# A hybrid decoder layer on one core: a third PSUM bank in the expert stage, rounded slot weights, later LayerNorm rows, and TensorE waits for its own last matmul

## The chip, the cores and the metric

The kernel runs on one core of one Trainium2 chip (trn2). The metric is the device time of one execution in microseconds; before the change it is the median of three timed runs. One more execution was recorded by the hardware profiler; its times are read below.

## The reference, cut to what matters

One decoder layer on 256 tokens of 2048 channels, all in float32:

```python
u = x @ w_in                      # conformer GLU | q k v | short conv | 3 gates
a   = silu(LN(conv31(a_val * sigmoid(a_gate))))
att = dilated window attention over 3 patterns, merged by softmax denominators
c   = cb * conv3(cc * ch)
merged = sum_n sigmoid(g_n) * (branch_n @ w_branch[n])
x = LN(alpha * x + merged @ w_out)
# MoE: 64 SwiGLU experts of width 256, sigmoid scores, 4 of 8 groups, top 8, one shared expert
x = LN(alpha * x + moe(x))
```

## The kernel before, in words

All engines run their own instruction streams; semaphores set the order, which is written out by hand. `x_hi`/`x_lo`, `h_hi`/`h_lo`, `y_hi`/`y_lo` and `w_hi`/`w_lo` are a float32 value rounded to float32r and the rest that the rounding leaves; products of such pairs stand for a float32 product.

**The mixer** (to about 1200 us). SP loads weights in 2 MiB pieces into two buffers `raw` (L491), ScalarE rounds them (L640), VectorE subtracts for the rest (L921), and TensorE multiplies. The work is 200 *units* in eleven segments (`qk0`, `v0`, `aval`, `agate`, `qk1`, `v1`, `cc`, `ch`, `cb`, `gb`, `out`). A unit is 16 pairs of one 512-column and one 256-column matmul (L1494 and L1495, or L1485 and L1487, L1468 and L1469). Its last matmul increments `s_mm`; before a unit TensorE waits for the split (`s_lo`) and a free PSUM bank (`s_ev`). `multiply` holds this; the first iteration of each segment is written out, the others run in a hardware loop. Matmul instructions are queued, so TensorE normally runs from one unit into the next. Attention and two channel sums of the conformer branch are placed between units of `aval`, `cc`, `ch` and `cb`.

At the segment `out`, POOL waits for `s_mm` at `BASE_OUT`, loads x into `acc` (L597), waits until `merged` is split (`s_mlo` 4), and then issues the broadcasts of the LayerNorm's gain and bias rows (L599, L600), the router bias, and two small tables. VectorE needs the rows in `normalize`.

**The experts** (from about 1261 us). Pairs of experts (p), two pairs to a *quad* (q), 16 quads, and at the end a *job* (one more pair for experts that have over 64 tokens; more jobs only where needed). Each pair has six weight units of 2 MiB in a ring of six buffers: four gate and up units (`gate_up`, L1711), two down units (`down`, L1744). SP issues a load (L521) when TensorE has finished the unit that held the slot. Per quad TensorE does, in this order:

1. gate and up of the first pair into `ps_proj[0]`;
2. combine of the quad before (`combine`, L1762): its rows, rounded and rest, spread to the tokens by a 0/1 matrix, in two halves of four chunks of four matmuls; VectorE adds each chunk to `acc` (L1286);
3. between the halves the transposes of the hidden rows (`turn_hidden`, L1721), after them those of the selection (`turn_select`, L1726);
4. down of the first pair into `ps_s`;
5. gate and up of the second pair into `ps_proj[1]`;
6. gather of the next quad's tokens (`gather_part`, L1664) in two halves of four chunks of eight matmuls, each copied out by ScalarE (L794), with `turn_hidden` between them;
7. the slot weights (`slot_weights`, L1673): selection transposed times the four routing weights, in float32, copied out by VectorE (L1261);
8. down of the second pair.

PSUM has `ps_proj` (2 banks), `ps_s` (4 banks) and `ps_t` (2 banks, `swing[0]` and `swing[1]`). Everything of steps 2, 3, 6 and 7 goes through the two banks of `ps_t`, so each takes its turn after the others' readers (`s_acc`, `s_xt`, `s_ht`, `s_spreadt`).

Of the kernel before, what the change touches and what calls it, by code (L numbers as in the profile page):

```python
# [5 lines left out]
P = 128  # L6
# [45 lines left out]
def build(nc, x, w_in, conv_a_w, conv_a_b, ln_a_g, ln_a_b, conv_c_w, w_branch, w_out, ln1_g, ln1_b,  # L52
# [29 lines left out]
    with ctx:  # L82
# [95 lines left out]
        quad_w = at("quad_w", [P, TT, 4], F32, 197.25)  # L178
        slot_w = at("slot_w", [P, 2], F32, 197.28125)
# [32 lines left out]
        def gather_swing(t):  # L212


            return t % 2 if t < 4 else (t + 1) % 2
# [331 lines left out]
        def _(pool):  # L547
# [50 lines left out]
            pool.wait_ge(s_mlo, 4)  # L598
            pool.dma_start(ln_g[:, :], ln1_g.to_broadcast([P, D])).then_inc(s_lnp, 16)  # L599
# [17 lines left out]
        def _(act):  # L617
# [172 lines left out]
            def take_gathered(q, first):  # L790

                for t in range(first, first + 4):
                    act.wait_ge(s_gathered, 8 * q + t + 1)
                    nc.scalar.activation(xt[:, 2 * t:2 * t + 2, :].rearrange("p a c -> p (a c)"), swing[gather_swing(t)],  # L794
                                         ACT.Copy).then_inc(s_xt, 1)
# [14 lines left out]
            def take_spread(n):  # L810

                act.wait_ge(s_spread, n + 1)
                nc.scalar.activation(spread_t[:, :, :], swing[1].rearrange("p (k c) -> p k c", k=2),
# [12 lines left out]
            take_gathered(0, 0)  # L826
            act.wait_ge(s_shturn, 1)
            nc.scalar.activation(sh_ht[:, :, :], swing[0].rearrange("p (f c) -> p f c", f=FT), ACT.Copy).then_inc(s_shht, 1)
            take_gathered(0, 4)

            def quad(q):

                silu(2 * q, 0)
                take_hidden(2 * q)
                take_spread(q)
                take_rows(2 * q, 0)
                silu(2 * q + 1, 1)
                take_gathered(q + 1, 0)
                take_hidden(2 * q + 1)
                take_gathered(q + 1, 4)  # L840
# [5 lines left out]
            def job_spread(i):  # L846

                act.wait_ge(s_spread, QUADS + i + 1)
                nc.scalar.activation(spread_t[:, 0, :], swing[1][:, 0:TOK], ACT.Copy).then_inc(s_spreadt, 1)
# [3 lines left out]
            job_spread(0)  # L853
# [7 lines left out]
            def one_job(i):  # L861
# [5 lines left out]
                job_spread(i)  # L867
# [18 lines left out]
        def _(dve):  # L886
# [357 lines left out]
            def select_quad(q, turned):  # L1244

                if turned:
                    dve.wait_ge(s_spread, q)
                for tt in range(TT):
# [4 lines left out]
                nc.vector.tensor_copy(quad_w[:, :, :], weight[:, :, bass.ds(4 * q, 4)]).then_inc(s_select, 1)  # L1253

            def weights_of_slots(q):
# [24 lines left out]
            def add_up(n, tt):  # L1280

                for c in range(4):
# [3 lines left out]
                    nc.vector.tensor_tensor(cols, swing[(c + tt) % 2], cols, ALU.add).then_inc(s_acc, 1)  # L1286
# [641 lines left out]
```

## Time and profile before

| | us |
|---|---|
| timed runs, median (lowest to highest) | 2267.52 (2263.24 to 2269.39) |
| the profiled execution, whole | 2277.95 |
| its span | 2276.2 |
| TensorE matmul busy | 2228.0 (98%) |
| VectorE, ScalarE, POOL busy | 1042.0, 703.4, 49.1 |
| read from HBM | 640.34 MB |

A matmul's end in the record is modelled and matmuls overlap, so "busy" does not say that TensorE runs at its peak; the distance from one matmul's start to the next says more. The chain of waits is followed back from the last instruction. An idle time in brackets is that of the engine before the row, with what ended it.

### The profile page before, as it was taken

Reading aid. Unit: us, or ns where it says so; the run is one execution under the profiler, and the core shown is the slowest. Engines: PE = TensorE matmul, PEld = TensorE weight load, DVE = VectorE, ACT = ScalarE, POOL = GpSimd, SP = SyncE. Lnnn points to the kernel's source line nnn. Section 1 sums busy time; section 2 is a strip of 40 time slices with the busy share of each in tenths; the row PEclk is TensorE's granted clock in tenths of the full one; section 3 lists DMA queues with packets and bytes.
Section 4 is the critical chain, followed back from the end, with each engine's and each line's share of the span. In section 5 each row is a group of like instructions: output and inputs, shape, how many; then the busy total and the mean of one; then the engine's idle time right before and its main releaser. Section 6 shows DMA issues by size and latency. Waiting matters only on the chain.

```text
span 2276.2 us, 34624 instructions
## 1 busy us (share of the span) xinstructions
PE 2228.0 (98%) x14218; PEld 1704.3 (75%) x14218; DVE 1042.0 (46%) x1311; ACT 703.4 (31%) x782; POOL 49.1 (2%) x56
## 2 busy tenths in 40 slices
PE   8999999999999999999999999999999999999997
PEld 7888888888888888888888666666666666666663
DVE  5444559986575666666663322222122111221224
ACT  4334443334444444444424111111111111111112
POOL 0000000000000000000100000000000000000000
PEclk9999999999999999999999999999999999999999
DMA  8555455555355555555755899999999999999994
GB/s 262 187 181 185 148 171 177 185 170 185 113 186 182 185 185 186 186 186 182 256 194 222 338 421 422 422 422 419 417 418 413 414 415 413 410 416 415 418 410 187
DMA packets 250666, 643.37 MB, mean 283 GB/s; under 512 B 5173, under 2 KB 185397, under 8 KB 198378
## 3 DMA queue, kind: packets, MB, share of 16 engines
q1 hardware_dynamic: 249578, 635.61, 73.2%
q0 software_dynamic: 880, 6.32, 0.7%
q8 instruction: 47, 0.77, 0.1%
q10 hardware_dynamic: 144, 0.52, 0.1%
q14 instruction: 17, 0.14, 0.0%
HBM read 640.34 MB, written 2.10 MB: 282 GB/s over the span
## 4 chain that ended last, share of the span: by engine, by line
PE 94%; DVE 3%; DMA 1%; ACT 1%; issue 1%; DVEq 0%; SPq 0%; ACTq 0%
PE ps_proj L1494 22%; PE ps_proj L1711 20%; PE ps_proj L1495 11%; PE ps_s L1744 10%; PE ps_t L1664 6%; PE ps_t L1762 6%; PE ps_s L1485 4%; PE ps_s L1487 2%; PE ps_t L1468 2%; PE ps_s L1468 2%; PE ps_proj L1623 1%; DMA raw<-in_w_out_dram 1%; PE ps_t L1469 1%; PE ps_s L1469 1%; PE ps_t L1528 1%
## 5 line engine op out<-in xcount | busy, mean ns | idle before, releaser
L1494 PE MATMUL ps_proj<-x_both,w_both 128*128 128x512 f32 x2144 | 758.8, 399 | 0.0
L1495 PE MATMUL ps_proj<-x_both,w_both 128*128 128x256 f32 x2144 | 601.8, 281 | 0.0
L921 DVE TENSOR_TENSOR w_both<-raw,w_both 128x2048 fp32r<-128x2048 f32 x196 | 472.3, 2410 | 210.3 <-ACT w_both L640 209.9
L1494 PEld LDWEIGHTS ps_proj<-x_both,w_both 128*128 128x128 f32 x2144 | 402.7, 188 | 99.1
L1711 PE MATMUL ps_proj<-ring,xt 128*64 128x256 f32 x4224 | 461.5, 379 | 0.0
L1711 PEld LDWEIGHTS ps_proj<-ring,xt 128*64 128x64 f32 x4224 | 305.1, 137 | 164.9 <-issue 19.0
L1495 PEld LDWEIGHTS ps_proj<-x_both,w_both 128*128 128x128 f32 x2144 | 405.0, 189 | 0.1
L640 ACT ACTIVATE w_both<-raw 128x2048 fp32r<-128x2048 f32 x196 | 373.7, 1910 | 90.6 <-PE ps_proj L1495 44.6
L1744 PE MATMUL ps_s<-ring,ht 128*64 128x512 f32 x1056 | 233.9, 595 | 0.1
L1269 DVE SCALAR_TENSOR_TENSOR hidden<-ps_proj,slot_w,gate_sig 128x256 f32<-128x256 f32 x33 | 16.0, 484 | 354.8 <-ACT gate_sig L802 344.0
L1277 DVE TENSOR_TENSOR y_lo<-ps_s,y_hi 128x1024 fp32r<-128x1024 f32 x64 | 75.4, 1219 | 222.1 <-ACT y_hi L820 222.1
L1744 PEld LDWEIGHTS ps_s<-ring,ht 128*64 128x64 f32 x1056 | 73.3, 137 | 134.8 <-issue 134.5
L802 ACT ACTIVATE gate_sig<-ps_proj 128x256 f32<-128x256 f32 x33 | 12.7, 386 | 407.9 <-PE ps_proj L1711 407.9
L1485 PE MATMUL ps_s<-w_both,x_both 128*128 128x512 f32 x384 | 136.1, 399 | 2.0 <-DVE w_both L921 2.0
L820 ACT ACTIVATE y_hi<-ps_s 128x1024 fp32r<-128x1024 f32 x64 | 62.1, 1023 | 218.5 <-PE ps_s L1744 218.5
L1664 PE MATMUL ps_t<-select,h_hi 128*128 128x256 f32 x544 | 112.8, 289 | 7.7 <-ACT xt L794 7.7
L1762 PE MATMUL ps_t<-y_hi,spread_t 128*128 128x512 f32 x256 | 106.9, 417 | 9.5 <-DVE acc L1286 9.5
L1286 DVE TENSOR_TENSOR acc<-ps_t,acc 128x512 f32<-128x512 f32 x128 | 88.4, 692 | 52.1 <-PE ps_t L1762 52.1
L1664 PE MATMUL ps_t<-select,h_lo 128*128 128x256 f32 x544 | 109.0, 282 | 0.0
L1487 PE MATMUL ps_s<-w_both,x_both 128*128 128x256 f32 x384 | 107.8, 281 | 0.0
L794 ACT ACTIVATE xt<-ps_t 128x512 f32<-128x512 f32 x136 | 81.4, 599 | 66.1 <-PE ps_t L1664 66.1
L1762 PE MATMUL ps_t<-y_lo,spread_t 128*128 128x512 f32 x256 | 100.8, 394 | 0.0
(279 smaller groups left out, 2040.8 us busy)
## 6 DMA issues: line engine op xcount, KB each, us to landing
raw<-in_w_in_dram SPq DMA_DIRECT2D x79, 2048.0 KB, 8.5
ring<-in_w_gate_dram SPq DMA_DIRECT2D x64, 2048.0 KB, 12.7
ring<-in_w_up_dram SPq DMA_DIRECT2D x64, 2048.0 KB, 15.9
ring<-in_w_down_dram SPq DMA_DIRECT2D x64, 2048.0 KB, 9.7
raw<-in_w_branch_dram SPq DMA_DIRECT2D x12, 2048.0 KB, 7.9
raw<-in_w_out_dram SPq DMA_DIRECT2D x8, 2048.0 KB, 8.2
ring<-in_w_gate_dram SPq DMA_DIRECT2D x4, 1024.0 KB, 11.0
ring<-in_w_up_dram SPq DMA_DIRECT2D x4, 1024.0 KB, 14.3
```

The costliest lines, as they stand in the source:

```text
L640: nc.scalar.activation(split_hi(u, w), raw_half(u, w), ACT.Copy).then_inc(s_hi, 1)
L921: nc.vector.tensor_tensor(split_lo(u, w), raw_half(u, w), split_hi(u, w).bitcast(F32), ALU.subtract).then_inc(s_lo, 1)
L1286: nc.vector.tensor_tensor(cols, swing[(c + tt) % 2], cols, ALU.add).then_inc(s_acc, 1)
L1468: pe.matmul(sums, hi[:, t, cols], branch_both[:, :, t, :], start=(t == 0), stop=False)
L1485: pe.matmul(sums, m_hi[:, t, tt * P:(tt + 1) * P], both[:, :, :, t, :], start=(t == 0), stop=False)
L1487: ins = pe.matmul(sums[:, 0:2 * P], m_lo[:, t, tt * P:(tt + 1) * P], hi[:, :, t, :], start=False, stop=(t == KT - 1))
L1494: pe.matmul(sums[:, :], hi[:, t, :], x_both[:, :, t, :], start=(t == 0), stop=False)
L1495: ins = pe.matmul(sums[:, 0:TOK], lo[:, t, :], x_hi[:, t, :], start=False, stop=(t == KT - 1))
L1664: ins = pe.matmul(swing[gather_swing(t)][:, a * TOK:(a + 1) * TOK], h[:, tt, c:c + P], select[:, tt, :], start=(i == 0), stop=(i == 3))
L1711: ins = pe.matmul(ps_proj[k][a * SLOTS:(a + 1) * SLOTS, j // 2 * F:(j // 2 + 1) * F], xt[:, j % 2 * (KT // 2) + t, (2 * k + a) * SLOTS:(2 ...
L1744: ins = pe.matmul(y_bank[c][a * SLOTS:(a + 1) * SLOTS, :], ht[:, f, a * SLOTS:(a + 1) * SLOTS], w[:, a, c * 512:(c + 1) * 512], start=(f = ...
L1762: ins = pe.matmul(swing[(c + tt) % 2], spread_t[:, k, tt * P:(tt + 1) * P], y[:, c * 512:(c + 1) * 512], start=(i == 0), stop=(i == 2 * pa ...
```

## The change

1. **Third bank.** The turned hidden rows stay in `swing[0]`. Combine alternates between `swing[1]` and `ps_proj[1]` (`rows_banks`), gather between `swing[1]` and `ps_proj[0]` (`quad_banks`). The turned selection moves to `swing[0]` (in the first quad it stays in `swing[1]` and is made before the hidden rows, so ScalarE takes it first), the slot weights too. The waits between the halves fall away, `s_ht` is waited for after the second half, and `s_acc` 8q before the second pair's gate and up. The first gather and further jobs keep two banks of `ps_t`.
2. **Rounded slot weights.** `quad_w` holds the routing weights rounded to float32r and the rest; the selection is used as float32r; one matmul with eight columns takes the place of a float32 one with four. VectorE copies, subtracts, and adds the two parts with a reduction in place of a copy.
3. **Later LayerNorm rows.** POOL waits for `s_mm` at `BASE_OUT + 6` before the two row broadcasts.
4. **Seven waits.** Before seven units of the mixer (first iterations only) TensorE waits until its own earlier work is done.

```diff
+        first_banks = [swing[(t if t < 4 else t + 1) % 2] for t in range(8)]
+        quad_banks = [swing[1], ps_proj[0][:, :]] * 4
+        rows_banks = [swing[1], ps_proj[1][:, :]] * 4
+        job_banks = swing * 4
...
             pool.wait_ge(s_mlo, 4)
+            pool.wait_ge(s_mm, BASE_OUT + 6)
             pool.dma_start(ln_g[:, :], ln1_g.to_broadcast([P, D])).then_inc(s_lnp, 16)
...
                 silu(2 * q, 0)
+                if is_first(q):
+                    take_spread(q)
                 take_hidden(2 * q)
-                take_spread(q)
+                if not is_first(q):
+                    take_spread(q)
...
+                w = weight[:, :, bass.ds(4 * q, 4)]
+                nc.vector.tensor_copy(quad_w[:, :, 0, :], w).then_inc(s_select, 1)
...
-                nc.vector.tensor_copy(quad_w[:, :, :], weight[:, :, bass.ds(4 * q, 4)]).then_inc(s_select, 1)
+                dve.wait_ge(s_select, 4 * q + 1)
+                nc.vector.tensor_tensor(quad_w[:, :, 1, :], w, quad_w[:, :, 0, :].bitcast(F32), ALU.subtract
+                                        ).then_inc(s_select, 1)
...
-                        nc.vector.tensor_copy(slot_w[rows, k:k + 1], swing[1][rows, 4 * k + 2 * k + a:4 * k + 2 * k + a + 1]
-                                              ).then_inc(s_slotw, 1)
+                        parts = bank[rows, 8 * k:8 * k + 8].rearrange("p (h e) -> p e h", h=2)
+                        nc.vector.tensor_reduce(slot_w[rows, k:k + 1], parts[:, 2 * k + a, :], AX_X, ALU.add
+                                                ).then_inc(s_slotw, 1)
...
+            def start_empty(name, j, u):
+                if (name, j) in (("qk0", 3), ("qk1", 0), ("gb", 0)):
+                    pe.wait_ge(s_mm, u.n)
+                elif (name, j) == ("out", 1):
+                    pe.wait_ge(s_mm, u.n - 1)
+                elif (name, j) == ("agate", 0):
+                    pe.wait_ge(s_av, HALF)
+                elif (name, j) == ("ch", 0):
+                    pe.wait_ge(s_asum, 1)
+                elif (name, j) == ("cb", 0):
+                    pe.wait_ge(s_asum, 2)
...
                 pe.wait_ge(s_lo, u.n + 1)
+                if isinstance(i, int) and i == 0:
+                    start_empty(name, j, u)
...
-                        ins = pe.matmul(swing[1][:, 4 * k:4 * k + 4], select[:, tt, k * P:(k + 1) * P].bitcast(F32),
-                                        quad_w[:, tt, :], start=(tt == 0), stop=(tt == TT - 1))
+                        ins = pe.matmul(bank[:, 8 * k:8 * k + 8], select[:, tt, k * P:(k + 1) * P],
+                                        quad_w[:, tt, :, :], start=(tt == 0), stop=(tt == TT - 1))
...
-                    combine(8 * (q - 1), 0, 2)
-                    pe.wait_ge(s_acc, 8 * (q - 1) + 3)
+                    combine(8 * (q - 1), 0, 2, rows_banks)
+                if is_first(q):
+                    turn_selects(swing[1])
                 turn_hidden(p)
                 if not is_first(q):
-                    pe.wait_ge(s_acc, 8 * (q - 1) + 4)
+                    combine(8 * (q - 1), 1, 2, rows_banks)
                     pe.wait_ge(s_ht, p + 1)
-                    combine(8 * (q - 1), 1, 2)
-                    pe.wait_ge(s_acc, 8 * (q - 1) + 7)
-                for k in range(2):
-                    for tt in range(TT):
-                        ins = turn_select(k, tt)
-                ins.then_inc(s_spread, 1)
+                    turn_selects(swing[0])
...
                     pe.wait_ge(s_hidden, p - 1)
+                    pe.wait_ge(s_acc, 8 * q)
...
                 if is_first(q):
-                    pe.wait_ge(s_ht, 1)
                     pe.wait_ge(s_spreadt, 1)
-                else:
-                    pe.wait_ge(s_acc, 8 * q)
-                    pe.wait_ge(s_spreadt, q + 1)
-                gather_part(q + 1, 0)
-                pe.wait_ge(s_xt, 8 * (q + 1) + 3)
+                gather_part(q + 1, 0, 4, quad_banks)
+                pe.wait_ge(s_spreadt, q + 1)
                 turn_hidden(p)
-                pe.wait_ge(s_xt, 8 * (q + 1) + 4)
-                gather_part(q + 1, 4, 1)
+                gather_part(q + 1, 4, 4, quad_banks)
                 pe.wait_ge(s_ht, p + 1)
-                gather_part(q + 1, 5, 3)
-                slot_weights(q + 1)
+                slot_weights(swing[0])
```

The same edits are made in the job behind the last quad (combine through `rows_banks`, its selection in `swing[0]`).

## Rows read from the trace of the kernel before

**Rows 1.** The page: busy time by engine, and the chain that ended last by engine

```profile
PE 2228.0 (98%) x14218; PEld 1704.3 (75%) x14218; DVE 1042.0 (46%) x1311; ACT 703.4 (31%) x782; POOL 49.1 (2%) x56
...
PE 94%; DVE 3%; DMA 1%; ACT 1%; issue 1%; DVEq 0%; SPq 0%; ACTq 0%
```

**Rows 2.** Chain in order of time, one quad of experts; columns: start, length in us, what

```profile
1450.16 4.05 PE ps_t L1762 x16
1455.07 4.08 PE ps_t L1762 x16
1459.66 7.02 PE ps_s L1744 x32
...
1480.49 4.02 PE ps_t L1664 x32
...
1489.27 0.79 PE ps_t L1673 x8
...
1510.89 4.05 PE ps_t L1762 x16
```

**Rows 3.** Timeline at the two gaps, TensorE and VectorE; idle before in brackets

```profile
1453.81 0.39 PE L1762 MATMUL ps_t<-y_lo,spread_t 128*128 128x512 f32 x1
1454.06 0.44 PE L1721 MATMUL ps_t<-ident,hidden 128*128 128x128 f32 x2
1455.07 0.47 PE L1762 MATMUL ps_t<-y_hi,spread_t 128*128 128x512 f32 x1 [0.57 <-DVE acc L1286]
...
1484.34 0.38 PE L1721 MATMUL ps_t<-ident,hidden 128*128 128x128 f32 x2
1485.19 0.51 PE L1664 MATMUL ps_t<-select,h_hi 128*128 128x256 f32 x2 [0.47 <-ACT xt L794]
...
1452.25 0.69 DVE L1286 TENSOR_TENSOR acc<-ps_t,acc 128x512 f32<-128x512 f32 x1 [0.23 <-PE ps_t L1762]
```

**Rows 4.** Windows, one quad each: length, busy us (count) by engine, clock, DMA share, GB/s

```profile
1328.70:1389.43 60.73, 59.69 (x433) 37.85 (x433) 12.59 (x21) 10.71 (x17) 0.00 (x0) 1.00 1.01 421
1450.16:1510.89 60.73, 59.69 (x434) 37.84 (x433) 12.59 (x21) 10.71 (x17) 0.00 (x0) 1.00 1.01 422
1935.99:1996.74 60.75, 59.71 (x435) 37.86 (x433) 12.60 (x21) 10.72 (x17) 0.00 (x0) 1.00 1.00 411
```

**Rows 5.** Loads L521 issued at 1275.4 and 2178.9: to landing; chain rows of their products

```profile
DMA to landing us min/median/max: 14.9/14.9/14.9
...
DMA to landing us min/median/max: 16.9/16.9/16.9
...
1284.47 13.81 PE ps_proj L1711 x128
2195.84 13.81 PE ps_proj L1711 x128
```

**Rows 6.** Loads L491 issued at 1117.4 and 1142.9; TensorE's stall; a wait of ScalarE

```profile
DMA to landing us min/median/max: 16.5/16.5/16.5
...
DMA to landing us min/median/max: 8.0/8.0/8.0
...
1142.93 0.47 PE L1485 MATMUL ps_proj<-w_both,merged_hi 128*128 128x512 f32 x1 [2.47 <-DVE w_both L921]
...
ACT w_both L640 <- PE ps_proj L1487: 10.1, 1, 10.1
```

**Rows 7.** Windows of two mixer stretches, TensorE alone: length, busy (matmuls), clock, DMA share, GB/s

```profile
655.00:1138.00 483.00, 483.00 (x2735) 1.00 0.57 191
607.00:648.00 41.00, 41.00 (x239) 1.00 0.52 172
```

**Rows 8.** Timeline of TensorE at two starts after idle in the mixer

```profile
489.20 0.28 PE L1487 MATMUL ps_s<-w_both,x_both 128*128 128x256 f32 x1
490.43 0.47 PE L1485 MATMUL ps_s<-w_both,x_both 128*128 128x512 f32 x1 [0.95 <-DVE w_both L921]
...
525.80 0.47 PE L1485 MATMUL ps_s<-w_both,x_both 128*128 128x512 f32 x1 [1.09 <-DVE w_both L921]
```

More of the change, by code:

```diff
@@ L1285, in add_up @@
                     cols = acc[:, tt, c * 512:(c + 1) * 512]
-                    nc.vector.tensor_tensor(cols, swing[(c + tt) % 2], cols, ALU.add).then_inc(s_acc, 1)
+                    nc.vector.tensor_tensor(cols, banks[4 * tt + c], cols, ALU.add).then_inc(s_acc, 1)
             def select_job(i):
@@ L1370, in one_job @@
                     rows = slice(a * SLOTS, (a + 1) * SLOTS)
-                    nc.vector.tensor_copy(slot_w[rows, 0:1], swing[0][rows, a:a + 1]).then_inc(s_slotw, 1)
+                    parts = swing[0][rows, 0:8].rearrange("p (h e) -> p e h", h=2)
+                    nc.vector.tensor_reduce(slot_w[rows, 0:1], parts[:, a, :], AX_X, ALU.add).then_inc(s_slotw, 1)
                 dve.wait_ge(s_slotw, 4 * (QUADS + 1) + 2 * i)
@@ L1650, in _, with gather_part @@
             shared_in(1, 1).then_inc(s_unit, 1)
-            def gather_part(q, first, n=4):
+            def gather_part(q, first, n, banks):
                 for t in range(first, first + n):
-                    if t >= 2 and t != 5:
-                        pe.wait_ge(s_xt, 8 * q + (t - 1 if t < 4 else t - (1 if t < 6 else 1)))
+                    if t >= 2:
+                        pe.wait_ge(s_xt, 8 * q + t - 1)
                     for a in range(2):
@@ L1722, in turn_hidden, with turn_select, turn_selects @@
                 ins.then_inc(s_hturned, 1)
-            def turn_select(k, tt):
-                return pe.transpose(swing[1][:, k * TOK + tt * P:k * TOK + (tt + 1) * P],
+            def turn_select(k, tt, bank):
+                return pe.transpose(bank[:, k * TOK + tt * P:k * TOK + (tt + 1) * P],
                                     select[:, tt, k * P:(k + 1) * P].bitcast(F32), ident[:, :])
+            def turn_selects(bank):
+                for k in range(2):
+                    for tt in range(TT):
+                        ins = turn_select(k, tt, bank)
+                ins.then_inc(s_spread, 1)
             def down(p, j, landed, count, by_chunk=False, more=False):
@@ L1748, in down, with combine @@
                 ins.then_inc(s_unit, 1)
-            def combine(n, tt, pairs):
+            def combine(n, tt, pairs, banks):
                 for c in range(4):
                     u = n + 4 * tt + c
-                    if c >= 2:
+                    if 4 * tt + c >= 2:
                         pe.wait_ge(s_acc, u - 1)
-                    elif tt and c == 0:
-                        pe.wait_ge(s_acc, u)
                     i = 0
@@ L1761, in combine @@
                         for y in (y_hi[k], y_lo[k]):
-                            ins = pe.matmul(swing[(c + tt) % 2], spread_t[:, k, tt * P:(tt + 1) * P], y[:, c * 512:(c + 1) * 512],
+                            ins = pe.matmul(banks[4 * tt + c], spread_t[:, k, tt * P:(tt + 1) * P], y[:, c * 512:(c + 1) * 512],
                                             start=(i == 0), stop=(i == 2 * pairs - 1))
```

86 lines of the change are left out of this document (42 added, 44 removed).

## The prediction

> **What bounds the kernel now.** I read the page first. TensorE is busy 98% of the span, and 94% of the chain that ended last is its work; VectorE and ScalarE are under half busy [rows 1]. The granted clock is 1.00 (2.4 GHz) in every stretch read below [rows 4, 7]. So time can go only where TensorE stands idle or does a step more slowly than it can. I therefore read the chain in order of time over a quad of experts, the DMA share by quad, and the mixer's matmul rate by stretch.
>
> The chain repeats every 60.73 us (1450.16 to 1510.89). The first half of the combine ends at 1454.21 and the second begins at 1455.07, 0.86 us later; that one ends at 1459.15, and 0.51 later the down product begins [rows 2]. The timeline names the stops: TensorE waits 0.57 for an accumulator add after the turned hidden rows, and 0.47 for a ScalarE copy between the halves of the gather [rows 3]. Both are waits for one of the two banks of `ps_t`.
>
> **The third bank.** The hidden rows and the turned selection get a bank of their own, and combine and gather swing between `ps_t`'s other half and an idle `ps_proj` bank.
> - Combine. From the last matmul of the first half (1453.81) to the first of the second (1455.07) are 1.26 us [rows 3]. What must stay is one matmul pitch (4.05 over 16 [rows 2], 0.25) and two transposes (four take at most the 0.51 before the down product [rows 2], so 0.25 at most, 0.22 taken). That is 0.79 less. The turned selection no longer waits for the last add, and the first matmul after a stop loses a little; for both together I take 0.14: 0.93. It happens in 15 quads and in the job: 16 x 0.93 = 14.9.
> - Gather. The first transpose is at 1484.34, the next gather matmul at 1485.19 [rows 3]; 0.22 must stay, so 0.63, with the restart 0.72. 16 x 0.72 = 11.5. Bounds of both sums together: the idle alone, 16 x 1.04 = 17, and 27.
> - Late next inside the halves: VectorE's add, 0.69 [rows 3], against four matmuls, 1.0. Two alternating banks suffice there, as they do now.
>
> **The rounded slot weights.** Eight records in 0.79 us [rows 2] become four. The trace has no such matmul with eight columns. The nearest rows are one-record transposes at some 0.11 (0.45 for four) and the old price. I take 0.45: 0.34 less, 17 times, 5.8 in all; at worst 0. The extra VectorE copy and subtraction and the reductions in place of copies lie beside TensorE's 13.81 us products and cost nothing: VectorE is busy 12.6 us of a quad [rows 4]. Without that cover it would be under a microsecond a quad.
>
> TensorE alone would so save 32.2 us, 1.0 per pair of experts: a quad would take 58.75 us.
>
> **What is late next: the weights.** A quad loads twelve units of 2 MiB, 25.17 MB. While the ring is being filled the DMA engines show a share of 1.01 at 421 to 422 GB/s, and only 411 later, with the loads far ahead [rows 4]. At 422 a unit takes 4.97 us and a quad 59.64 (59.78 at 421), more than 58.75. The loads' lead covers the difference only for a while. The last gate and up unit of the second pair landed at 1275.4 + 14.9 = 1290.3; TensorE began it three quarters into its product, at 1284.47 + 10.36 = 1294.8, 4.5 later. The same unit of the last pair, 180 loads on, landed at 2178.9 + 16.9 = 2195.8 and was begun at 2195.84 + 10.36 = 2206.2 [rows 5]. Unbroken, those 180 loads end at 1290.3 + 894.6 = 2184.9. So there TensorE can be at most 21.3 us earlier (19.4 at 421 GB/s), although its own saving would be 30. Behind it the job's weights allow 0.55 more, and the job's combine gives 0.93; the first slot weights, 0.34, lie before the loads start. The experts: 21.3 + 0.55 + 0.93 + 0.34 = **23.1 us**.
>
> The Trainium skill ("HBM Reference", section "Specifications (TRN2)") also speaks against the full gain: a core that streams alone measures about 425 GB/s, bounded by its 16 DMA engines. By that figure, an estimate, a quad would take 59.2 us and the experts would give some 29. The rate in the rows is lower, 421 to 422 [rows 4], and decides.
>
> **The LayerNorm rows.** Their two 1 MiB broadcasts go out just before a `w_out` load issued at 1117.4, which takes 16.5 us to land where a later one takes 8.0; TensorE then stands 2.47 us before the block at 1142.93 [rows 6]. After the change they go out three product pairs later, near 1140. The load then lands near 1128 and the stall goes: **-2.5**. The load that they meet instead has slack: ScalarE waits 10.1 us for TensorE before it splits the next one [rows 6]. Without that slack the stall would only move: bounds -2.5 and +2.5. VectorE wants the rows some 40 us after they land. The small table work queued behind them on POOL moves too and is wanted only after the normalization.
>
> **The seven waits.** Each empties TensorE before a block. The nearest row is the start at 490.43, after a wait for VectorE: 0.95 idle, 1.23 from the last matmul's start [rows 8]. A wait for TensorE's own end has only the pipeline's end and the semaphore in it; I take half of the 0.95, 0.47 each, 3.3 together. Bounds: 0 (where TensorE waits anyway) and 7 x 0.95 = 6.7.
>
> They may also change the pace. At the same clock the mixer's matmul pair runs in one of two steady paces: 2735 matmuls in the 483 us from 655 to 1138, 353 ns per pair; 239 in the 41 us from 607 to 648, which is 346 without the two that straddle the edges [rows 7]. The stretches from 30 to 235 and from 287 to 487 run like the first, the one from 1144 to 1198 like the second. The pace changes only where the stream is interrupted. The slow pace costs 1.9% of 888 us, 16.6 us. Does an empty start give the fast pace? After 490.43 and 525.80 [rows 8] the stream stayed slow, after 1142.93 [rows 6] it became fast. The profile does not decide it. I take half, **-8.3**; the ends are -16.6 and, if the fast stretches turned slow, +1.8.
>
> **The sum.** -23.1 - 2.5 + 3.3 - 8.3 = -30.6 us on the profiled 2277.95 us (span 2276.2, and 1.75 around it): 2247. The median of the three timed runs is 2267.52, 10.4 lower; the same amount off it gives **2237 us**.
>
> **Rivals.**
> 1. The DMA limit does not bind, because loads run faster when no profile is taken: 32.2 in place of 23.1, so 2228. For it: the timed runs are quicker than the profiled one. Against: the share is already 1.01. The skill's 425 GB/s lies between the two: about 2231.
> 2. All seven starts give the fast pace: 8.3 more, 2229. For it: each wait starts the stream at a fixed distance from TensorE's own end, so all may fall alike. The opposite, none fast, is 2245, or 2247 with the fast stretches lost.
> 3. The waits for banks only change their names (copies and adds become the limit, the slot weights cost as before): the experts give 10 to 15 instead of 23: 2245 to 2250. Against it: 0.69 against 1.0.
> 4. Slower than before: with a dry ring every pair pays idle DMA time, since SP issues a load only when TensorE has freed its slot. For it: the late quad at 411 instead of 422 GB/s lost 1.6 us, 0.8 per pair [rows 4]. At 1.2 us per pair a pair would take 31.0 instead of 30.4, 21 us over 32 pairs; with the other terms (-7.5) 2281. It decides from 0.8 per pair on. Against: the early quads, 4.5 us ahead, lose nothing; the late ones lose because the ring is full.
>
> **Chances.** The forecast 0.48; rivals 1 and 2 together 0.27; no start fast, and rival 3, 0.20; rival 4 0.02; an effect of the rows or waits that I have not seen 0.03. The range 2223 to 2249 cuts only the tails of the first three. Runs of this kernel can be told apart by about 0.3%, 7 us: faster 0.95, same 0.03, slower 0.02.
>
> **What would show it.** Right: no idle between the halves of combine and gather; 0.45 for the slot weights; share 1.01 and 421 to 422 GB/s in all quads; quads of 58.75 at first and 59.7 from about the twelfth pair on, with new waits of TensorE for gate and up weights; the `w_out` load landing in 8 to 11 us; pairs of 346 ns behind some of the seven waits. Wrong: quads of 60.7, or of 58.75 to the end, or a stall of TensorE behind the moved rows.

## The result, and the profile after

| | before | after |
|---|---|---|
| median of 5 runs, us | 2267.52 (2263.24 to 2269.39) | 2257.78 (2253.87 to 2259.46) |
| ratio | 1 | 0.9957, 95% interval 0.9941 to 0.9972 |
| profiled execution, us | 2277.95 | 2259.46 |
| from the first gate and up product to the end | 1014.85 | 993.53 |
| from the start to that product | 1261.28 | 1264.04 |

The time before is the median of five runs, not of three as said ahead of the prediction. The kernel became 9.7 us faster. I had forecast 30.5. The profiled executions differ by 18.5: 21.3 less in the experts, 2.8 more in the mixer.

The page of the changed kernel, the rows that answer to [rows 1]. TensorE was 94% of the chain; now transfers of weights hold 27% of it. That is the length of the transfers on the chain, not idle time: TensorE's matmuls wait for them 8.4 us in all, 1.3 at most at a time.

```profile
PE 2219.7 (98%) x14150; PEld 1697.6 (75%) x14150; DVE 1043.9 (46%) x1329; ACT 702.7 (31%) x782; POOL 50.3 (2%) x56
...
PE 71%; DMA 27%; DVE 1%; issue 0%; ACT 0%; DVEq 0%; SPq 0%; ACTq 0%
```

The chain in order of time over an early quad, beside [rows 2] (start, length, what). Combine and gather run without a stop in two banks. From combine to down product are 8.52 us, which were 9.50; the gather's two halves with their two transposes take 8.05, which were 8.78; the slot weights take 0.34 instead of 0.79.

```profile
1447.42 1.13 PE ps_t L1793 x4
...
1450.53 0.93 PE ps_proj L1793 x4
1451.45 0.22 PE ps_t L1747 x2
1451.67 0.93 PE ps_t L1793 x4
...
1455.51 0.44 PE ps_t L1752 x4
1455.94 7.02 PE ps_s L1777 x32
...
1476.77 1.15 PE ps_t L1690 x8
...
1484.82 0.34 PE ps_t L1698 x4
1485.16 7.02 PE ps_s L1777 x32
```

The same chain late in the loop. Each pair of experts now waits for its fourth load, and TensorE's last quarter of the product follows it. The row at 2188.86 belongs to the last pair, the one behind it to the job's loads.

```profile
2131.75 26.06 DMA ring<-in_w_up_dram
2157.81 0.04 issue
2157.85 3.70 PE ps_proj L1737 x32
2161.57 27.25 DMA ring<-in_w_up_dram
2188.81 0.04 issue
2188.86 3.70 PE ps_proj L1737 x32
...
2193.00 25.76 DMA ring<-in_w_up_dram
```

Windows of one quad each, as in [rows 4]: 58.57 us while TensorE sets the pace, 59.6 when the loads do. The share stays at 1.01 and the rate at 422 GB/s to the end.

```profile
1447.42:1505.99 58.57, 58.57 (x429) 37.41 (x429) 12.66 (x22) 10.70 (x17) 0.00 (x0) 1.00 1.01 422
1535.00:1594.60 59.60, 59.03 (x432) 37.22 (x428) 12.66 (x22) 10.70 (x17) 0.00 (x0) 1.00 1.01 422
1935.00:1994.60 59.60, 58.97 (x432) 37.22 (x429) 12.66 (x22) 10.68 (x17) 0.00 (x0) 1.00 1.01 422
```

In the mixer the stall of [rows 6] is gone. A window of the output product after (TensorE's busy time is the second number) has 0.1 us without work, and the `w_out` load issued at 1107.8 lands in 8.1 us.

```profile
1110.00:1200.00 90.00, 89.90 (x509) 77.78 (x509) 56.97 (x60) 27.28 (x17) 7.27 (x9) 1.00 0.68 237
```

```profile
DMA to landing us min/median/max: 8.1/8.1/8.1
```

One of the seven waits, ahead of the block at 333.81. The wide matmul would have started 0.12 us behind the narrow one of 333.43; it starts 0.38 behind it, and its first narrow one 0.31 instead of 0.23 later: 0.33 us in all. The seven together cost 2.3 us, from 0.3 to 0.5 each.

```profile
333.43 0.28 PE L1524 MATMUL ps_proj<-x_both,w_both 128*128 128x256 f32 x1
333.81 0.47 PE L1523 MATMUL ps_proj<-x_both,w_both 128*128 128x512 f32 x1
334.12 0.28 PE L1524 MATMUL ps_proj<-x_both,w_both 128*128 128x256 f32 x1
```

And the pace, as in [rows 7]: 2283 matmuls in the long stretch are 353 ns per pair, and the stretch that was fast is slow too.

```profile
705.00:1108.00 403.00, 403.00 (x2283) 1.00 0.55 182
610.00:652.00 42.00, 42.00 (x240) 1.00 0.52 170
```

So in this trace the waits made no long stretch fast. That explains 8.3 us of the miss. It does not explain why the profiled execution gained 18.5 us and the median only 9.7. The experiments were made for that.

### The profile page after: what moved, and what is told of

It is laid out like the page before. It is cut to its first block, busy times and chain, and to the rows that moved or that the text cites. A ratio compares the mean times of both kernels' runs of the same rounds, so it can differ in the third digit from the quotient of the medians.

```text
span 2257.6 us, 34431 instructions
## 1 busy us (share of the span) xinstructions
PE 2219.7 (98%) x14150; PEld 1697.6 (75%) x14150; DVE 1043.9 (46%) x1329; ACT 702.7 (31%) x782; POOL 50.3 (2%) x56
## 4 chain that ended last, share of the span: by engine, by line
PE 71%; DMA 27%; DVE 1%; issue 0%; ACT 0%; DVEq 0%; SPq 0%; ACTq 0%
DMA ring<-in_w_up_dram 27%; PE ps_proj L1523 22%; PE ps_proj L1524 11%; PE ps_proj L1737 10%; PE ps_s L1514 4%; PE ps_s L1777 3%; PE ps_s L1516 2%; PE ps_t L1497 2%; PE ps_s L1497 2%; PE ps_proj L1652 1%; PE ps_t L1690 1%; PE ps_s L1498 1%; PE ps_t L1498 1%; PE ps_proj L1514 1%; PE ps_t L1793 1%; PE ps_proj L1793 1%
## 5 line engine op out<-in xcount | busy, mean ns | idle before, releaser
L1737 PE MATMUL ps_proj<-ring,xt 128*64 128x256 f32 x4224 | 466.6, 380 | 8.4 <-DMA ring<-in_w_up_dram 8.4
L1074 DVE SCALAR_TENSOR_TENSOR branch<-a_pad,par,branch 128x256 f32<-128x256 f32 x240 | 97.2, 469 | 0.0
L1514 PEld LDWEIGHTS ps_s<-w_both,x_both 128*128 128x128 f32 x384 | 72.1, 188 | 20.7 <-issue 3.0
L1516 PEld LDWEIGHTS ps_s<-w_both,x_both 128*128 128x128 f32 x384 | 72.5, 189 | 0.0
L1270 DVE TENSOR_REDUCE slot_w<-ps_t 64x1 f32<-64x2 f32 x68 | 10.7, 158 | 129.3 <-PE ps_t L1698 127.7
L673 ACT ACTIVATE gates<-gates 128x256 f32<-128x256 f32 x48 | 20.1, 418 | 159.4 <-DVE gates L1019 159.4
L1497 PE MATMUL ps_t<-branch_both,w_both 128*128 128x512 f32 x192 | 68.4, 399 | 0.0
```

The source lines that it names most:

```text
L1074: ins = nc.vector.scalar_tensor_tensor(out=y, in0=v, scalar=w, in1=y, op0=ALU.mult, op1=ALU.add)
L1497: pe.matmul(sums, hi[:, t, cols], branch_both[:, :, t, :], start=(t == 0), stop=False)
L1514: pe.matmul(sums, m_hi[:, t, tt * P:(tt + 1) * P], both[:, :, :, t, :], start=(t == 0), stop=False)
L1516: ins = pe.matmul(sums[:, 0:2 * P], m_lo[:, t, tt * P:(tt + 1) * P], hi[:, :, t, :], start=False, stop=(t == KT - 1))
L1737: ins = pe.matmul(ps_proj[k][a * SLOTS:(a + 1) * SLOTS, j // 2 * F:(j // 2 + 1) * F], xt[:, j % 2 * (KT // 2) + t, (2 * k + a) * SLOTS:(2 ...
```

## The experiments

The mixer has some 3170 such matmul pairs. In each profile I counted how many run in the fast pace (346.7 ns per pair) and how many in the slow one (353.3), and took the time of the first gate and up product and from there to the end. "Long stretches" are those that begin near 30, 285, 330, 605, 655, 700 and 1100 us (the two of 655 and 700 are one where no wait parts them).

| kernel | median us (runs) | profiled us | pairs fast, slow | mixer us | experts us |
|---|---|---|---|---|---|
| before | 2267.52 | 2277.95 | 367, 2800 | 1261.28 | 1014.85 |
| before, again | 2269.93 (12) | 2274.52 | 1023, 2149 | 1257.82 | 1014.89 |
| before with the waits | 2279.90 (12) | 2280.65 | 493, 2659 | 1263.94 | 1014.89 |
| after | 2257.78 | 2259.46 | 157, 3004 | 1264.04 | 993.53 |
| after, again | 2255.97 (6) | 2250.00 | 1314, 1856 | 1254.78 | 993.40 |
| after without the waits | 2243.52 (6) | 2236.58 | 2963, 214 | 1240.95 | 993.81 |
| experts' parts alone | 2247.43 (6) | 2246.16 | 2430, 737 | 1250.76 | 993.58 |
| only the wait at `gb` | 2250.32 (6) | 2246.20 | 1478, 1698 | 1250.76 | 993.62 |
| seven waits, matmuls added | 2257.66 (8) | 2244.08 | 2820, 348 | 1248.48 | 993.78 |
| the same, again | 2257.43 (1) | 2257.43 | 828, 2339 | 1261.73 | 993.88 |

Two things stand in it. In the profiles the experts take the same time for each kernel, and for all the changed ones here, to 0.5 us. The variation is in the mixer, and the slow pairs carry most of it: 2963 fast pairs against 367 are 17.2 us at 6.63 ns each, of the 20.3 us between the first and the sixth row (2.5 of the rest is the stall of [rows 6]). A second, smaller source lies in the first 21 us. The granted clock was 0.5 (1.2 GHz) there for 3.4 us in the first profile of the kernel before, for 6.8 us in the first of the changed kernel, and for no time in the profile without the waits; each 3.4 us at 0.5 cost about 1.5, since a pair then takes 0.64 us instead of 0.35.

**Without the seven waits.**

```diff
                 pe.wait_ge(s_lo, u.n + 1)
-                if isinstance(i, int) and i == 0:
-                    start_empty(name, j, u)
                 if by_pair(name):
```

> The changed kernel without the seven waits for TensorE's own last matmul; nothing else differs. Two theories of why the gain on the median (9.7 us) is about half the gain between the two profiled executions (18.5 us). Theory P (pace): the kernel before runs part of its mixer in the fast pace (346 ns per pair instead of 353) in many executions and none of it in others, the waits pin nearly all of it to the slow pace; then without the waits the median is lower by 7 us and more, about 2246 to 2251 against 2257.8, and the profile shows more than the two short fast stretches. Theory E (experts): the experts' stage gains less in the timed executions than in the profiled one, and the waits cost only their own 0.3 us each: then the median is 2254 to 2257 and the profile shows the pace of the kernel before (fast 610-652 and 1143-1197, slow elsewhere).

Median 2243.52 us (2236.58 to 2254.40), ratio to before 0.9892 (0.9862 to 0.9922). The profile has nearly the whole mixer in the fast pace, 2604 matmuls in 451 us of the longest stretch, 346 ns per pair. Theory P holds and was too timid: against the two medians of the changed kernel, 2257.78 and 2255.97, the waits cost 12 to 14 us. Set against the kernel before, timed beside each (0.9957, 0.9934 and 0.9892), it is 10 to 15.

```profile
647.00:1098.00 451.00, 451.00 (x2604) 1.00 0.56 187
```

**The kernel before with the seven waits alone.** The edit is the reverse of the one above, with the function `start_empty`, in the kernel before.

> The kernel before with the seven waits alone. Theory P: 5 to 10 us slower than the kernel before (2273 to 2278), because the fast stretches that the kernel before has in its timed executions go. Theory E: 2 us of waits and 1.8 us of lost fast stretches: 2269 to 2272.

Median 2279.90 us, ratio 1.0037 (1.0020 to 1.0055), twelve times from 2277.49 to 2281.70. Theory P again, and again too timid (it gave 2273 to 2278); the twelve times stand where the slowest ones of the kernel before do, and the spread of 15 us has shrunk to 4.

**The kernel before, once more.** No edit.

> The kernel before once more, unchanged, timed against itself: the ratio should be 1.000 within 0.002. The profile is what it is for: theory P expects that the stretches of fast and slow pace lie elsewhere than in the first profile, with a profiled time that differs from 2277.95 by several us for that reason; theory E expects the same stretches and a profiled time of 2276 to 2280.

Ratio 1.000 (0.998 to 1.002). In this execution the stretch from 29 to 233 us is fast (1179 matmuls in 204 us), which in the first profile was slow; the long one is slow again. So the pace of that stretch is not a property of the kernel. The profile on which the prediction rests showed an execution with nearly every stretch slow, and 2277.95 lies at the upper end of before's times.

```profile
651.00:1134.00 483.00, 483.00 (x2736) 1.00 0.58 191
...
29.00:233.00 204.00, 204.00 (x1179) 1.00 0.60 195
```

**The experts' parts alone**: third bank and rounded slot weights.

```diff
             pool.wait_ge(s_mlo, 4)
-            pool.wait_ge(s_mm, BASE_OUT + 6)
             pool.dma_start(ln_g[:, :], ln1_g.to_broadcast([P, D])).then_inc(s_lnp, 16)
...
-                if isinstance(i, int) and i == 0:
-                    start_empty(name, j, u)
```

> The changed kernel without the seven waits and with the LayerNorm rows at their old place: what is left is the third bank and the rounded slot weights, all in the experts. The terms of the prediction give -23.1 us on the kernel before: 2244.4 against 2267.5. Theory P: the full 20 to 23 us, 2244 to 2248. Theory E: 10 to 13 us, 2254 to 2258. The profile should show the 2.5 us stop of TensorE ahead of the output product's blocks again.

Median 2247.43 us, ratio 0.9905 (0.9874 to 0.9936), where theory P gave 2244 to 2248. The stop ahead of the output product is back: the waits of TensorE between 1095 and 1200 us (what waited for what: total us, times, longest) have this one row, and none at all in the run without waits, which has the rows at their later place.

```profile
PE ps_proj L1511 <- DVE w_both L924: 3.3, 1, 3.3
```

Behind this stop the granted clock was 0.5 for 3.4 us, and the pairs came 0.64 us apart until 1134.66, which is another 1.5 us. The kernel before with the waits had the same behind a stop of 2.2 us; the two profiles of the kernel before had a stop of 2.5 us and a granted clock of 1.00 behind it.

```profile
1131.37 0.76 PE L1511 MATMUL ps_proj<-w_both,merged_hi 128*128 128x512 f32 x1 [3.33 <-DVE w_both L924]
...
1132.14 0.63 PE L1511 MATMUL ps_proj<-w_both,merged_hi 128*128 128x512 f32 x1
...
1134.66 0.40 PE L1511 MATMUL ps_proj<-w_both,merged_hi 128*128 128x512 f32 x1
```

**Only the wait ahead of the longest stretch.**

```diff
-                if isinstance(i, int) and i == 0:
-                    start_empty(name, j, u)
+                if isinstance(i, int) and (name, i, j) == ("gb", 0, 0):
+                    pe.wait_ge(s_mm, u.n)
```

> The changed kernel without six of its seven waits; the one left stands ahead of the gate and branch units, the longest stretch (409 us). So far an empty start on TensorE's own end was slow each time that the stream before it was fast, and slow or fast after a slow one. So this one wait should turn the fast stretch of 450 us in which the kernel without waits runs in its quicker executions into a slow one: 7.6 us for the 1150 pairs in each such execution, a median of 2247 to 2251 against 2243.5, and the profile shows the long stretch slow. If the waits do nothing to the pace, 2243 to 2245.

Median 2250.32 us (2246.20 to 2252.09), 6.8 more than without it. The long stretches before it are fast; from the wait on 1407 pairs are slow (2708 matmuls in 478 us), which is 9.3 us at 6.63 ns each. The times alone do not settle it: the ratios to the kernel before, 0.9912 (0.9890 to 0.9934) and 0.9892 (0.9862 to 0.9922), overlap. That this wait of 0.33 us slows what follows rests on the traces.

```profile
692.00:1170.00 478.00, 478.00 (x2708) 1.00 0.58 195
599.00:640.00 41.00, 41.00 (x239) 1.00 0.52 171
28.00:232.00 204.00, 204.00 (x1178) 1.00 0.60 196
```

**The changed kernel, once more.** No edit.

> The changed kernel once more, unchanged. The experts from their first gate and up product to the end should take 993.5 us again; all that can vary is the mixer ahead of them. If the seven waits chain the paces (each start inherits its pace from the end of the stream before), the long stretches (36 to 237, 334 to 490, 704 to 1109, 1111 to 1200) are all slow again and the time is 2254 to 2260. If the slow paces of the first profile were a chance, some of them are fast now.

Median 2255.97 us, ratio 0.9934 (0.9910 to 0.9958). The expectation "all slow again" fell, though the median is the one it gave: the stretches behind 34, 329 and 650 us are fast now. Those behind 283, 601, 695 and 1102 us are slow again, and among them is the longest, although the stretch before it was fast. The six times lie at 2249.7 and 2250.0 and, four of them, between 2255.4 and 2257.6.

```profile
696.00:1099.00 403.00, 403.00 (x2283) 1.00 0.55 182
601.00:643.00 42.00, 42.00 (x239) 1.00 0.51 165
34.00:234.00 200.00, 200.00 (x1155) 1.00 0.59 191
```

**Many empty starts, with further waits behind them.** Two runs; the second has `+ 3`.

```diff
+            EMPTY = [("qk0", 3), ("v0", 1), ("v0", 3)] + [("agate", j) for j in range(4)]
+            EMPTY += [(n, j) for n in ("qk1", "ch", "cb") for j in range(4)] + [("gb", j) for j in range(8)]
             def start_empty(name, j, u):
-                if (name, j) in (("qk0", 3), ("qk1", 0), ("gb", 0)):
...
+                if (name, j) in EMPTY or (name, j) in (("out", 1), ("out", 3)):
+                    pe.wait_ge(s_mm, u.n - int(by_pair(name)))
+                    if (name, j) in EMPTY:
+                        for _ in range(EMPTY.index((name, j)) % 6):
+                            pe.wait_ge(s_const, 2)
```

> The changed kernel with an empty start (a wait for TensorE's own last matmul) ahead of 29 units of the mixer instead of seven blocks, and behind each wait 0 to 5 further waits that are already met, so many more sequencer steps, in turn (unit k of the list has k mod 6). Each unit is then a stream of its own whose pace the trace shows. Theory D (the distance from TensorE's own end to the start fixes the pace): the same number of further waits gives the same pace each time, all slow for none, and fast for some other number. Theory R (the pace is drawn anew at each start): fast and slow are mixed for each number. The time says little: 29 starts at 0.3 to 0.5 us are 9 to 15 us more than without them.

> As the run before, with the numbers of further waits shifted by three: unit k has (k + 3) mod 6. Theory D: the paces move with the numbers. A third theory, that the unit's place decides, expects the same paces at the same units as before. Theory R: mixed, and no relation to the run before.

The first matmuls (0.47 us long) of successive `gb` units of the first run, then of the second. A unit of 16 pairs lasts 5.99, 5.98 or 5.90 us, and these three follow each other in a fixed round, whatever the number of further waits (1, 2, 3, 4, 5, 0, 1, 2 in the first run, 4, 5, 0, 1, 2, 3, 4, 5 in the second). The one fast unit of each round is that of 5.90 or 5.89. Both theories fell: in these two runs neither the number of further waits nor a new draw decides, and what is left is what the stream before left behind. Twelve times in these two runs a stretch that was fast behind such a start ran straight into the next such start, and all twelve times the next stretch was slow. Behind a slow one came either.

```profile
706.05 0.47 PE L1521 MATMUL ps_proj<-x_both,w_both 128*128 128x512 f32 x1
...
712.04 0.47 PE L1521 MATMUL ps_proj<-x_both,w_both 128*128 128x512 f32 x1
...
718.02 0.47 PE L1521 MATMUL ps_proj<-x_both,w_both 128*128 128x512 f32 x1
...
723.92 0.47 PE L1521 MATMUL ps_proj<-x_both,w_both 128*128 128x512 f32 x1
```

```profile
704.51 0.47 PE L1521 MATMUL ps_proj<-x_both,w_both 128*128 128x512 f32 x1
...
710.50 0.47 PE L1521 MATMUL ps_proj<-x_both,w_both 128*128 128x512 f32 x1
...
716.39 0.47 PE L1521 MATMUL ps_proj<-x_both,w_both 128*128 128x512 f32 x1
...
722.38 0.47 PE L1521 MATMUL ps_proj<-x_both,w_both 128*128 128x512 f32 x1
```

The two runs also show the size: the last `gb` start of the first is slow and holds 1038 pairs, that of the second is fast; 2264.08 against 2254.01 us, one execution each. Of these 10.1 us, 7.3 are 1098 more slow pairs, and about 3 are 6.8 us at a granted clock of 0.5 at the start of the first, which the second does not have.

**Matmuls added ahead of the start**, instead of further waits.

```diff
                     sums = ps_proj[u.bank]
+                    if isinstance(i, int) and i == 0 and (name, j) in EMPTY:
+                        for kind in ((), ("wide",), ("wide", "wide"), ("narrow",), ("narrow", "narrow"),
+                                     ("narrow", "wide"))[EMPTY.index((name, j)) % 6]:
+                            if kind == "wide":
+                                pe.matmul(sums[:, :], hi[:, 0, :], x_both[:, :, 0, :], start=True, stop=True)
+                            else:
+                                pe.matmul(sums[:, 0:TOK], lo[:, 0, :], x_hi[:, 0, :], start=True, stop=True)
                     for t in range(KT):
```

> The same 29 empty starts without further waits, but with 0, 1 or 2 additional matmuls ahead of the unit's first one (unit k: none, one wide, two wide, one narrow, two narrow, narrow and wide by k mod 6); their sums are thrown away. Theory D: none gives slow every time, and at least one of the kinds gives fast every time, because it shifts the start against the engine's own end by a fixed amount. Theory R: mixed for each kind.

One execution, 2255.73 us. In the sixteen units from `ch` on, two narrow matmuls gave a slow stretch both times and every other kind a fast one. Nothing added gave a fast one too, three times, each after the unit with one narrow and one wide. Ahead of `ch` it is less clean: one narrow gave a slow unit at 283 us, and two narrow a fast one at 289 and a slow stretch at 348. So the added matmuls seem to shift the state, but the kinds stood in a fixed order and each met the state that the one before had left.

**One narrow and one wide matmul behind six of the seven waits**, added to the changed kernel.

```diff
+                    if isinstance(i, int) and i == 0 and (name, j) in (("qk0", 3), ("agate", 0), ("qk1", 0), ("ch", 0),
+                                                                       ("cb", 0), ("gb", 0)):
+                        pe.matmul(sums[:, 0:TOK], lo[:, 0, :], x_hi[:, 0, :], start=True, stop=True)
+                        pe.matmul(sums[:, :], hi[:, 0, :], x_both[:, :, 0, :], start=True, stop=True)
```

> The changed kernel with its seven waits, and behind six of them (all but the output product's) two additional matmuls, one of 256 and one of 512 columns, ahead of the unit's own; their sums are thrown away. Theory D' (from the runs before: an empty start after TensorE's own end inherits its pace from the state in which the stream before it ended, and these two matmuls turned the start to the fast pace 5 times of 5): most of the mixer runs at 346.7 ns per pair, up to 16 us less, and the twelve matmuls cost 2 us: 2242 to 2247 against 2257.8. Theory R (the pace is drawn anew, independent of the matmuls): about half of the stretches fast, 2248 to 2252 and a wide spread. Theory W (the waits themselves hold the engine slow): 2259 to 2260.

> The kernel with seven waits and two additional matmuls behind six of them, once more. Its eight times fell into two groups, 2242 to 2244 (twice) and 2257 to 2259 (six times), and the profile is of the first group. Expected from the second group (3 in 4): a profile at 2257 to 2259 with the long stretches behind 331, 652 and 697 us slow, the experts unchanged at 993.5 us. If instead the experts differ between the groups, the pace of the mixer is not what separates them.

The median of the first run is 2257.66 us, ratio 0.9942 (0.9924 to 0.9960). None of the three theories, but a clean split: two executions at 2242.12 and 2244.08 us, six from 2256.86 to 2258.96. The profile of one of the two has all long stretches fast but the one at 285 us. That of the second run, at 2257.43, has three of the others slow as well, those behind the first wait and behind the last two. Those at 334, 608 and 656 us are fast in it too, against what I expected. The windows, first run and then second:

```profile
698.00:1097.00 399.00, 399.00 (x2304) 1.00 0.56 185
604.00:646.00 42.00, 42.00 (x243) 1.00 0.52 169
```

```profile
703.00:1105.00 402.00, 402.00 (x2277) 1.00 0.55 183
608.00:650.00 42.00, 42.00 (x244) 1.00 0.53 170
333.00:488.00 155.00, 154.90 (x894) 1.00 0.56 182
```

So the stretches that begin near 36, 698 and 1098 us changed together, and the ones between them did not. With a few shorter ones, 1992 pairs more were slow: 13.2 us of the 13.35 between the two. The start at `gb` followed a fast stretch in both profiles and was fast once and slow once. So with the added matmuls the pace of the stretch before does not by itself fix the next one. Why the times fall into two groups, and what ties the first wait to the last two, stays open.

**The two matmuls at three places**: with the wait ahead of them, without it, and with the middle place moved from `agate` to `qk1`.

```diff
+                    if isinstance(i, int) and i == 0 and (name, j) in (("qk0", 3), ("agate", 0), ("cb", 0)):
+                        pe.matmul(sums[:, 0:TOK], lo[:, 0, :], x_hi[:, 0, :], start=True, stop=True)
+                        pe.matmul(sums[:, :], hi[:, 0, :], x_both[:, :, 0, :], start=True, stop=True)
```

> The same two matmuls at three places only, ahead of the three longest stretches (the fourth unit, the attention's gates, the second branch's sums), each behind its wait; the four other waits are gone. Theory D': the three stretches, 843 us, are fast in every execution, 2236 to 2240, and the spread is that of the changed kernel (5 us), not that of the one without waits (18 us). Theory R: as without waits, 2243.5 plus 2, with a spread of 15 us and more.

> The two matmuls at the same three places, and no wait for TensorE's own end anywhere. If the matmuls alone decide, 2235 to 2239 with a narrow spread; if the empty engine is needed for it, 2243.5 plus 1, with the wide spread of the kernel without waits.

> The changed kernel with three waits (the fourth unit, the second half's queries and keys, the second branch's sums), each followed by the two additional matmuls, and none elsewhere: like the run with three places, but the place ahead of the attention's gates, behind which 575 pairs came out slow, is given up for the one 42 us later, behind which 447 pairs came out fast. If these starts come out fast here too: 3 us less, 2240 to 2242. If the pace behind them depends on what the stream before left, 2242 to 2250 and two groups of times.

Medians 2243.92 (4 runs, 2243.65 to 2247.62), 2243.97 (4 runs, 2241.49 to 2245.64) and 2246.09 us (6 runs, 2239.32 to 2253.16); ratios 0.9886 (0.9861 to 0.9910), 0.9879 (0.9855 to 0.9903) and 0.9891 (0.9865 to 0.9917). All miss the forecast of 2236 to 2242: in each profile at least one long stretch is slow (near 285; near 35 and 1107; near 36, 333 and 1112). None can be told from the kernel without waits, 0.9892. (The forecast rested on five fast starts of five behind these two matmuls; the trace of the run before has four of four.) A start that is fast every time was not found.

**Fewer bytes for the experts.**

```diff
+                        m = slice(0, 2048 if isinstance(q, int) else 1792)
-                        sp.dma_start(ring[r][:, :, :], pair_source(j, bass.ds(2 * p, 2)).rearrange("e p m -> p e m")
+                        sp.dma_start(ring[r][:, :, m],
+                                     pair_source(j, bass.ds(2 * p, 2)).rearrange("e p m -> p e m")[:, :, m]
```

> The changed kernel without its seven waits, and in quads 1 to 14 of the experts each load brings 1792 of the 2048 columns (1.75 MiB instead of 2 MiB); the products read what the ring held before for the rest. Theory of the prediction (the weights' transfer is late next, at 4.97 us per 2 MiB): at 4.35 us per load TensorE is the limit again, every quad takes 58.5 to 58.6 us to the end of the loop, no wait of TensorE for gate and up weights, and the time is 8 to 10 us below the kernel without waits (2234 to 2236 against 2243.5). Rival (the later quads are slower for another reason, as traffic that shares SBUF with VectorE or the packets of the copies): 59.6 us per quad stay and the time does not move.

This kernel leaves out 256 of the 2048 columns of each of these loads and serves to see the time alone. Median 2228.42 us (2226.64 to 2240.86), where I expected 2234 to 2236. The experts take 979.96 us instead of 993.81: 13.9 less, where I expected 8 to 10. All quads last 58.57 us to the end (two windows), at a share of 0.94, and DMA is gone from the chain. The rival fell. The eleven late quads give 1.07 each and the job 1.9, which makes 13.7; my 8 to 10 was read too low.

```profile
1606.00:1664.57 58.57, 58.57 (x430) 37.49 (x429) 12.66 (x22) 10.69 (x18) 0.00 (x0) 1.00 0.94 377
1900.00:1958.57 58.57, 58.57 (x430) 37.50 (x429) 12.66 (x23) 10.68 (x17) 0.00 (x0) 1.00 0.94 377
```

The chain of the same run by engine, from its page:

```profile
PE 97%; DVE 1%; issue 0%; ACT 0%; DMA 0%; DVEq 0%; ACTq 0%
```

## Why the prediction was wrong

- **The experts, -23.1: measured -21.3, right in mechanism and nearly in size.** TensorE alone gives 2.16 us per quad where I took 1.99 (combine 0.98, gather 0.73, slot weights 0.45). The limit by the loads came much as worked out: the first ten pairs of experts at TensorE's pace, then 59.64 us per quad. At the last quarter of the loop's last product TensorE is 20.1 us earlier than before, where the working gave 21.3: the 180 loads took 895.8 us and not 894.6. The job's loads gave 0.25 more and not 0.55, and its combine 0.97, as forecast; together that is the 21.3. The first slot weights gave 0.45, but ahead of the first product, so outside this figure. The experts' terms so miss 1.3 us. The Trainium skill ("HBM Reference", section "Specifications (TRN2)") has 425 GB/s for a core that streams alone, which would make, as an estimate, 59.2 us per quad; the measured 59.64 at 422 decides.
- **The LayerNorm rows, -2.5: right.** No stall in any profile with the rows at their later place, loads at 8 to 11 us, and nothing late behind them. The two profiles of the kernel before have the stall of 2.5, and the one with the experts' parts alone 3.3.
- **The waits' own cost, +3.3: too high.** 0.33 us each on average, 2.3 in all.
- **The pace, -8.3: this is the step that failed**, and it failed twice. First, the forecast took half of the stretches as fast behind an empty start. In both profiles of the changed kernel the 1400 pairs behind its last two waits are slow, and the single wait at `gb` did the same to them. Against the kernel without waits the seven cost 12 to 14 us: 2.3 of their own, and 9.3 for the 1400 pairs behind the last two, which are fast in all three profiles of the changed kernel without waits or added matmuls.
- **Second, the step from the profiled time to the median.** I wrote that the profiled execution is 10.4 us above the median and took the same 10.4 off the forecast, as if it were the same for every kernel. It is not: the changed kernel's profiled time was 1.7 above its median, and in the later runs the profiled time stood between 4.6 above the median and 13.6 below it. The profiled execution of the kernel before had 2800 of 3167 pairs slow, which is nearly as slow as the pace can make it. So the profile overstated what there was to gain. That the timed executions were quicker because fewer of their pairs were slow is inferred, since only profiled executions have a trace; it fits the second profile of the same kernel, with 651 slow pairs fewer and 3.4 us less.
- **The miss of 20.8 us, added up.** The step to the median is 8.7, the pace term 8.3, lost fast stretches 1.4 (367 fast pairs became 157), the experts' terms 1.3. The start of the kernel took 2.0 longer: the first product began 0.7 later, and the granted clock was 0.5 for 6.8 us instead of 3.4. The waits' own cost (1.0 less) comes off. That makes 20.7.
- **Among the rivals**, number 2 had this case as its "opposite", 2245 to 2247, and the range ended at 2249, because the step to the median was taken as a constant in every case. Rivals 3 and 4 fell: combine and gather run without a stop, and the late quads take 59.6 us. Rival 1 speaks of loads when no profile is taken, which no run here can show.

Shown: the experts' time and its limit, by the run with fewer bytes; that the pace differs from execution to execution and, in the profiles, only in the mixer; that the seven waits cost 10 to 15 us, mostly through the pace. The traces show it for the one wait at `gb` too, but its times alone are not clear of noise. In the two runs with many starts a fast stretch was followed by a slow one twelve times of twelve; with added matmuls that did not always hold. That a start takes over a state of the stream before it is the reading that fits this best, and it is not proven. Open: what that state is in the engine; why the stretch behind 650 us was slow in both profiles of the kernel before and fast in three of three of the changed kernel without waits, though TensorE's code for the mixer is the same; and how a start could be made fast every time. The best version is the changed kernel without its waits, 2243.5 us, 1.1% below the kernel before.

## What to carry to other kernels

Before a profiled execution is taken as the base of a sum, compare its time with all the timed ones; if it lies at their edge, find which stage varies (two profiles of the same kernel side by side do it) and price that stage against the middle of the executions, not against the profile. A wait that "costs nothing" at 0.3 us can change the pace of the 400 us behind it, so test each added wait by itself. And when a stage gets shorter, work out when its loads become the bound: at a share of 1.01 they were already there, and the bandwidth sum gave TensorE's lead at the last product of the loop as 21.3 us, where 20.1 was measured.

## What the runs showed of the hardware

- Alternating f32r matmuls of 512 and 256 columns, all at a granted clock of 1.00 (2.4 GHz), run at 346.7 or at 353.3 ns per pair. The pace holds for over a thousand pairs and changed only where the stream was interrupted.
- It can differ between executions of one kernel: the kernel before was slow from 28 us on in one profile and fast there in the other, behind a restart on another engine's signal. Behind restarts on TensorE's own end, with no matmuls added, a fast stretch was followed by a slow one each time (twelve of twelve in the two runs with many starts). Units of 16 pairs went in a round of three (5.99, 5.98, 5.90 us).
- Additional waits, already met, did not move that round (0 to 5 of them). With additional matmuls other orders appeared.
- The granted clock was 0.5 (1.2 GHz) for 3.4 us behind a stop of TensorE of 3.3 us in one profile and of 2.2 us in another, and stayed at 1.00 behind one of 2.5 us in two; a pair takes 0.64 us at 0.5.
- 2 MiB loads in an unbroken row ran at 422 GB/s, 4.97 us each, for 890 us with VectorE, ScalarE and TensorE at work.
